# A mixture-of-experts stage on one core: gate and up products in 32-token groups on four column strips, and activations transposed on VectorE

## The reference

```
gate = jnp.minimum(xb @ w_gate[e] + b_gate[e], SWIGLU_LIMIT)
up = jnp.clip(xb @ w_up[e] + b_up[e], -SWIGLU_LIMIT, SWIGLU_LIMIT)
act = (up + 1.0) * gate * jax.nn.sigmoid(SWIGLU_ALPHA * gate)
return act @ w_down[e] + b_down[e]
```

## Time and profile before

| | |
|---|---|
| runs | 2298.77 us median of 3 (2298.28 to 2299.28) |
| span of the profiled execution | 2300.9 us |
| PE busy | 2168.5 us (94%) |
| DVE busy | 1023.7 us (44%) |
| ACT busy | 478.9 us (21%) |
| POOL busy | 452.8 us (20%) |
| HBM read, written | 482.08 MB, 32.51 MB |

### The profile page before, as it was taken

The page is one execution under the profiler, slowest core; times in us unless marked ns, Lnnn a source line. Parts: engine busy times, 40 slices in busy tenths (PEclk is TensorE's granted clock), DMA queues, the critical chain, the costliest instruction groups (busy, mean ns, idle before and its releaser), DMA issues.

```text
span 2300.9 us, 35458 instructions
## 1 busy us (share of the span) xinstructions
PE 2168.5 (94%) x9927; PEld 1011.6 (44%) x9928; DVE 1023.7 (44%) x1591; ACT 478.9 (21%) x647; POOL 452.8 (20%) x422
## 2 busy tenths in 40 slices
PE   6999999789959999999999899999999999999995
PEld 3544444564534444443443344444444444444442
DVE  2765656657772432534335243433254333222346
ACT  2343347422210111111011111111111111111134
POOL 0011100002321222323122232212213212212212
PEclk9999999889969999999999999999999999999998
DMA  9222320022245776789479999747899647897673
GB/s 352 80 63 76 101 73 19 3 107 87 82 193 186 263 271 221 268 305 393 146 281 399 351 353 402 268 162 252 300 373 345 235 160 261 292 320 247 206 280 130
DMA packets 169785, 512.34 MB, mean 223 GB/s; under 512 B 16815, under 2 KB 51383, under 8 KB 168586
## 3 DMA queue, kind: packets, MB, share of 16 engines
q1 hardware_dynamic: 152290, 468.96, 54.7%
q0 software_dynamic: 15840, 37.45, 7.3%
q10 hardware_dynamic: 1608, 5.29, 0.6%
HBM read 482.08 MB, written 32.51 MB: 224 GB/s over the span
## 4 chain that ended last, share of the span: by engine, by line
PE 87%; DVE 5%; DMA 3%; SPq 2%; issue 2%; ACT 1%; POOLq 0%; POOL 0%; DVEq 0%; ACTq 0%
PE psall L587 27%; PE psall L615 14%; PE psall L591 10%; PE psall L772 9%; PE psall L596 5%; PE psall L619 5%; PE psall L760 3%; PE psall L879 2%; PE psall L873 2%; PE psall L624 2%; DMA arena<-in_w_down_dram 2%; PE psall L656 1%; PE psall L739 1%; SPq L437 1%; DVE arena L1498 1%
## 5 line engine op out<-in xcount | busy, mean ns | idle before, releaser
L587 PE MATMUL psall<-arena 128*128 128x512 f32 x1472 | 645.5, 597 | 23.9 <-issue 18.7
L587 PEld LDWEIGHTS psall<-arena 128*128 128x128 f32 x1472 | 278.6, 191 | 369.2 <-issue 362.5
L615 PE MATMUL psall<-arena 128*128 128x512 f32 x736 | 322.6, 596 | 4.8 <-issue 2.7
L591 PE MATMUL psall<-arena 128*64 128x512 f32 x1152 | 256.1, 595 | 6.2 <-issue 2.5
L1670 DVE STREAM_TRANSPOSE arena<-arena 128x1024 f32<-128x1024 f32 x49 | 61.0, 1246 | 447.4 <-PE psall L587 276.5
L772 PE MATMUL psall<-arena 128*128 128x512 f32 (+1 forms) x560 | 227.1, 562 | 0.0
L615 PEld LDWEIGHTS psall<-arena 128*128 128x128 f32 x736 | 139.2, 191 | 182.6 <-issue 180.8
L1256 ACT COPY arena<-psall 128x512 f32<-128x512 f32 x49 | 28.7, 586 | 729.1 <-PE psall L656 729.1
L1869 DVE COPY arena<-psall 128x512 f32<-128x512 f32 x48 | 33.2, 692 | 310.7 <-PE psall L656 303.0
L1268 ACT ACTIVATE arena<-arena 128x1024 f32<-128x1024 f32 x49 | 51.8, 1057 | 569.3 <-DVE arena L1697 556.0
L1652 DVE TENSOR_TENSOR arena<-psall,arena 32x256 f32<-32x256 f32 (+2 forms) x122 | 78.6, 644 | 195.5 <-PE psall L615 137.5
(11 more groups left out here) (332 smaller groups left out, 2130.4 us busy)
## 6 DMA issues: line engine op xcount, KB each, us to landing
arena<-in_w_gate_dram SPq DMA_DIRECT2D x128, 1024.0 KB
arena<-in_w_up_dram SPq DMA_DIRECT2D x128, 1024.0 KB
arena<-in_w_down_dram SPq DMA_DIRECT2D x128, 1024.0 KB
arena<-in_w_ada_dram SPq DMA_DIRECT2D x16, 1024.0 KB, 5.2
arena<-in_w_ada_dram SPq DMA_DIRECT2D x4, 2048.0 KB, 14.7
arena<-in_x_dram SPq DMA_DIRECT2D x16, 512.0 KB, 6.8
arena<-in_w_in_dram SPq DMA_DIRECT2D x16, 512.0 KB, 4.0
arena<-in_w_out_dram SPq DMA_DIRECT2D x1, 4096.0 KB, 13.8
```

The lines of the kernel that those rows point to most:

```text
L587: mm = pe.matmul(ps[2 * g + s], xT[:, k, :], w[:, s * BANK:(s + 1) * BANK], start=(k == 0), stop=(k == KD - 1))
L591: mm = pe.matmul(ps[2 * g][HT * j:HT * j + HT, :], xT[:, k, 0:HT], w[:, j * BANK:(j + 1) * BANK], start=(k == 0), stop=(k == KD - 1), skip ...
L615: mm = pe.matmul(ps[6 + s], aT[:, k, :], w[:, s * BANK:(s + 1) * BANK], start=(k == 0), stop=(k == KD - 1))
```

## The change

PE computes gate and up for every kind in the same way. The tokens are taken in groups of 32. For a group t, the four quarters of the hidden columns go to the four column strips, and the moving operand of one product is 256 gate columns and 256 up columns together, 512 in all, read as two pieces (`wpair`, which is the ring seen as four pairs of a gate and an up piece). The result of a group fills one PSUM bank, gate in the first half and up in the second (`psGU`, four banks). Kind 4 has 128 such products where it had 32, kind 3 has 96, kind 2 has 64 and kind 1 has 32.

DVE then adds the biases with one instruction each over 256 columns a group, on all 128 partitions, for every kind. The activations stay in strips: partition 32j+s, column 256t+n holds token 32t+s and hidden column 256j+n. `turn_activations` transposes them in 32x32 blocks with a read step of eight columns, so that partition p of `aT` holds hidden columns 8p to 8p+7. The down weights are loaded to match: eight consecutive rows of `w_down` on each partition, two of them a piece, in runs of 8 KB. PE's transposes, their PSUM banks and the copies of ACT and DVE are gone.

The order within a turn is new. PE: gate and up of job u in one block, then down of job u-1. The block begins when both sums of job u-1 have been read from PSUM (`gu_free`), where before the gate part waited for `g_biased` alone and the up part for `gu_free`. DVE: rows of the next job, `swiglu` of u, `weigh` of u-1, and then the turn of the activations of u, since `aT` is in use until the down product of u-1 ends. PE gives a gate and an up piece free together. SP issues the gate and up pieces of the next expert first, then waits for `gu_free` and loads its two bias rows straight to 128 partitions (`ebq`: quarter j of the row to partitions 32j to 32j+31, 1 KB each), then the down pieces. POOL broadcasts the down bias row alone.

```diff
+        ebq = reg(o, 2, QW); o += 512
+        ebd = reg(o, D); o += 1024
...
+        wpair = [reg(4096 * m, 2, 2, D) for m in range(NPAIR)]
+        brow = adarow[0:1, 2, :]
...
-        psG, psU = psall[:, 0:2 * BANK], psall[:, 2 * BANK:4 * BANK]
-        psT, psY = psall[:, 4 * BANK:6 * BANK], psall[:, 6 * BANK:8 * BANK]
+        psGU = psall[:, 0:4 * BANK].rearrange("p (t g n) -> p t g n", t=4, g=2)
+        psY = psall[:, 6 * BANK:8 * BANK]
...
-                    if u is not None:
-                        sp.wait_ge(gu_used, GUP * u + (q + 1))
+                    if u is not None and q % 2 == 0:
+                        sp.wait_ge(gu_used, NPAIR * u + (q // 2 + 1))
...
-                    w_v = w_down[0].rearrange("e (q c p) n -> e q p c n", c=2, p=P)[:, q]
+                    w_v = w_down[0].rearrange("e (p q c) n -> e q p c n", q=DNP, c=2)[:, q]
...
-                    sp.dma_start(brow[:, g * D:(g + 1) * D], b_v[0][ds(e, 1)]).then_inc(d_bias, 16)
+                    rows = b_v[0][ds(e, 1)].rearrange("a (j n) -> (a j) n", j=4)
+                    sp.dma_start(ebq[:, g], rows.unsqueeze(1).to_broadcast([4, QR, QW])).then_inc(d_bias[g], 16)
...
-                            spread = sp.value_load(tab[0:1, ds(u * NC + (NC + J_ORD), 1)], min_val=16, max_val=16 * NE)
-                            sp.wait_ge(bias_spread, spread)
-                            settle(sp)
+                            gu_pieces(e, u)
+                            sp.wait_ge(gu_free, u + 2)
                             bias_rows(e)
-                            gu_pieces(e, u)
...
-        def gate_up(pe, kind, u, order_, k0, k1, first=False):
-            if k0 == 0:
+        def gate_up(pe, groups, u, order_, m0, m1):
+            if m0 == 0:
                 pe.wait_ge(xT_ready, u + 1)
-            sweeps = {4: ("full",), 3: ("half", "quarter"), 2: ("half",), 1: ("quarter",)}[kind]
-            for sweep in sweeps:
-                for q in range(k0, k1):
-                    g = q % 2
-                    if q < 2 and sweep == sweeps[0]:
-                        if g == 0 and not first:
-                            pe.wait_ge(g_biased, u)
-                        if g == 1:
-                            pe.wait_ge(gu_free, u + 1)
-                    if sweep == sweeps[0]:
-                        pe.wait_ge(d_gu[q], order_)
-                        if kind < 4:
-                            settle(pe)
-                    for k in (2 * (q // 2), 2 * (q // 2) + 1):
-                        w = ring[q][:, k % 2]
-                        if sweep == "full":
-                            for s in range(2):
-                                mm = pe.matmul(ps[2 * g + s], xT[:, k, :], w[:, s * BANK:(s + 1) * BANK],
-                                               start=(k == 0), stop=(k == KD - 1))
-                        if sweep == "half":
-                            for j in range(2):
-                                mm = pe.matmul(ps[2 * g][HT * j:HT * j + HT, :], xT[:, k, 0:HT], w[:, j * BANK:(j + 1) * BANK],
-                                               start=(k == 0), stop=(k == KD - 1), skip_group_check=True)
-                        if sweep == "quarter":
-                            r = slice(QUARTER_AT[kind], QUARTER_AT[kind] + QR)
-                            for j in range(4):
-                                mm = pe.matmul(ps[2 * g + 1][QR * j:QR * j + QR, 0:QW], xT[:, k, r], w[:, j * QW:(j + 1) * QW],
-                                               start=(k == 0), stop=(k == KD - 1), skip_group_check=True)
-                    if sweep == sweeps[-1]:
-                        mm.then_inc(gu_used, 1)
+                pe.wait_ge(gu_free, u + 1)
+            for m in range(m0, m1):
+                for q in (2 * m, 2 * m + 1):
+                    pe.wait_ge(d_gu[q], order_)
+                    settle(pe)
+                for k in (2 * m, 2 * m + 1):
+                    for t in range(groups):
+                        for j in range(4):
+                            mm = pe.matmul(psGU[QR * j:QR * j + QR, t], xT[:, k, QR * t:QR * t + QR],
+                                           wpair[m][:, :, k % 2, QW * j:QW * j + QW],
+                                           start=(k == 0), stop=(k == KD - 1), skip_group_check=True)
+                mm.then_inc(gu_used, 1)
 
         def down(pe, kind, u, order_):
-            pe.wait_ge(aT_act, u + 1)
-            pe.wait_ge(aT_dve, u + 1)
+            pe.wait_ge(aT_ready, u + 1)
...
                             t, on_ = typ_of(pe, typ_c), ord_of(pe, ord_c, wait_c)
-                            by_kind(pe, t, lambda kind: gate_up(pe, kind, u, on_, 0, GUP // 2))
+                            by_kind(pe, t, lambda kind: gate_up(pe, kind, u, on_, 0, NPAIR))
                             tp, op_ = typ_of(pe, typ_p), ord_of(pe, ord_p, wait_p)
-                            with pe.If(tp > 0):
-                                pe.wait_ge(act_ready, u + 1)
-                                by_kind(pe, tp, lambda kind: turn(pe, ub, JOB_KINDS[kind][2] // P, JOB_KINDS[kind][1] // P).then_inc(act_turned, 1))
-                                pe.nop()
-                            by_kind(pe, t, lambda kind: gate_up(pe, kind, u, on_, GUP // 2, GUP))
                             job_row(pe, [typ_n, ord_n], u + 2)
                             by_kind(pe, tp, lambda kind: down(pe, kind, u, op_))
...
-            def swiglu(u, kind):
-                parts, lo, hi = JOB_KINDS[kind]
+            def swiglu(u, groups):
                 s7 = 1.0 / (1.0 + math.exp(-SWIGLU * LIMIT))
-                dve.wait_ge(gu_used, u * GUP + GUP)
-                dve.wait_ge(bias_spread, order_)
-                for p0, p1, c, b, n in parts:
-                    mm = dve.tensor_tensor(gb[p0:p1, c:c + n], psG[p0:p1, c:c + n], ebias[p0:p1, 0, b:b + n], ALU.add)
-                mm.then_inc(g_biased, 1)
-                for p0, p1, c, b, n in parts:
-                    mm = dve.scalar_tensor_tensor(out=ub[p0:p1, c:c + n], in0=psU[p0:p1, c:c + n], scalar=1.0,
-                                                  in1=ebias[p0:p1, 1, b:b + n], op0=ALU.add, op1=ALU.add)
-                mm.then_inc(gu_free, 1)
-                w = slice(lo, hi)
+                w = slice(0, QW * groups)
+                gv, uv = (v[:, w].rearrange("p (t n) -> p t n", t=groups) for v in (gb, ub))
+                bias = [ebq[:, g].unsqueeze(1).to_broadcast([P, groups, QW]) for g in range(2)]
+                dve.wait_ge(gu_used, u * NPAIR + NPAIR)
+                dve.wait_ge(d_bias[0], order_)
+                dve.tensor_tensor(gv, psGU[:, 0:groups, 0], bias[0], ALU.add).then_inc(g_biased, 1)
+                dve.wait_ge(d_bias[1], order_)
+                dve.wait_ge(aT_ready, u + 1)
+                dve.scalar_tensor_tensor(out=uv, in0=psGU[:, 0:groups, 1], scalar=1.0, in1=bias[1],
+                                         op0=ALU.add, op1=ALU.add).then_inc(gu_free, 1)
                 dve.wait_ge(gu_free, u + 2)
...
+            def turn_activations(u, groups):
+                dve.wait_ge(act_ready, u + 2)
+                dve.wait_ge(dn_used, u * DNP + DNP)
+                dve.transpose(aT[:, :, 0:QR * groups].rearrange("p b (t s) -> p t b s", s=QR),
+                              ub[:, 0:QW * groups].rearrange("p (t i b) -> p t b i", i=QR, b=KD)).then_inc(aT_ready, 1)
...
                                     by_kind(dve, tp, lambda kind: weigh(u, kind, orderp))
+                                    by_kind(dve, typ_of(dve, typ_c), lambda groups: turn_activations(u, groups))
```

65 lines of the change are left out of this document (21 added, 44 removed).

## The result

| | us, median (range) | runs |
|---|---|---|
| before | 2298.65 (2298.28 to 2299.28) | 4 |
| after | 2773.0 (2761.53 to 2792.16) | 4 |
| ratio | 1.2067, 95% interval 1.2028 to 1.2106 | |

The account below looks back on a forecast made before the run. PE's own work bounds most of the expert stage, the weights' arrival some 200 us. -7-37-6+2+2+3+8+4 = -31 off the 2298.77 us median gave 2268 us, own range 2254 to 2280, overall 2250 to 2318.

Parts of the forecast that it names:

- the loop, once fetched, stays with the engine: PE's job loop: no instruction packets after 780 us in the profile before, so no refetching; 0 us in the sum.
- Rival A: PE's grown loop is refetched every pass: +32 (2300 us) with one packet, +130 (near 2398) with several; chance 0.10 each.
- The price of a fetch: Instruction packet of 16 KB for PE: put at 2 us, an estimate between 0.7 us and three times it.
- The bias rows: Gate and up bias to 128 partitions, 0.7 us an expert by DMA; +4 with the later request of the first down piece.
- my terms ahead of it: Products -7, PE transposes -37, issue gaps -6, DVE's turn +2, start +2, waits for weights +8.
- The 8 for weights: Full DMA stretches, where PE's savings only make it wait for weights: +8 us given back.
- The rate of four strips: PE's gate and up products, 512 columns on four strips: 108 ns an instruction, 112 as upper bound; products -7 us.
- rival B: PE's strips slow each other at 512 columns, 112 ns an instruction: 2307 us, slower; chance 0.07.
- The issue gaps: PE's waits for branches and table loads ahead of blocks: -6 of 18 us, between 0 and -12.
- The end: Last down block, now behind weigh of the job before and the turn (1.25 us) on DVE: +3 us.
- Rival C: Saturated weight stretches widen, by pairwise ring release or bias packets on few engines: another 12 to 20, 2283 us; chance 0.14.
- The 144 groups of 32: Token groups from 288 transposes at two per 32 tokens, used to get 8, 10 and 8 jobs of kinds 3, 2, 1.

Follow-up runs that it names:

- after_3as4: The changed kernel with kind 3 running kind 4's gate and up products in the loop, its own code removed; 2352.17 us, ratio 1.0222.
- after_cut: The changed kernel without one never-executed piece of code ahead of the loop, which then starts 69 instructions earlier; 2701.96 us, ratio 1.172.
- before_pad24: The kernel before with 24 never-executed products (96 instructions) added in the job loop; 2972.99 us, ratio 1.2933.
- before_pad88: The kernel before with 88 never-executed products (352 instructions) added in the job loop; 3047.58 us, ratio 1.3257.
- one_code: The changed kernel with one code for all kinds' gate and up products, groups 1 to 3 behind tests of the kind; 2330.71 us, ratio 1.0121.
- bias_wide: one_code with the bias rows brought in by eight requests of 32 partitions in place of two of 128; 2302.26 us, ratio 1.0.
- bias_late: one_code with the bias rows and the wait for gu_free moved behind the down pieces on SP's queue; 2316.84 us, ratio 1.0062.
- bias_none: one_code without the gate and up bias rows of all experts but the first, and without waits for them; 2271.06 us, ratio 0.9861.

## Why the prediction was wrong

**The step that failed** is that the loop, once fetched, stays with the engine. Rival A named the mechanism and the point from which it decides, and the packets of 256 in the loop (5.9 to 7.1) were worked out, but it got a chance of 0.20 in all, on the ground that nothing shows where the store ends. The rule cited there from the Trainium skill ("Runtime: NRT & Kernel Launch", "Instruction fetch mechanics") gives a store of 2048 instructions in blocks of 256; by that the loop and one block ahead are 9 blocks where 8 fit. The runs bear it out to the block: loops of 7 blocks stay (before, after_3as4), loops of 8 don't (after, after_cut, before_pad24), and before_pad24 and before_pad88 fetch, in the mean of all passes, their blocks and nearly one more. In the prediction's own terms, the sum had 0 for instruction fetches, and they cost 442 us. Rival A ought to have been the forecast.

**The size of rival A** was off in one factor. The price of a fetch was put at 2 us and measures 1.5 to 1.8. The count was put at one or two a pass, "at each jump"; it is 4.9 in the mean, and 8.9 in before_pad24, where nearly every block is entered in every pass: a loop that is one block too long loses more than the block that doesn't fit. 248 x 1.78 = 442 us, not 130.

**The bias rows** are the term of the sum that was mis-sized: +4, measured 61 in one_code. I priced their packets by their share of 16 engines, 0.7 us an expert. Not in that price: the few packets under way at a time (30 us, bias_wide), and SP's wait for VectorE and its two requests (7.7 us for the pair at 1060 us), both in front of the down pieces (16 together, bias_late). The remaining part of the 61 is not divided. The rule of the Trainium skill ("DMA: Bandwidth & Descriptors", section on why a DMA increments its semaphore by 16) by which 4 source rows go to 4 engines, which I had set at 12 to 15 us and left out of the sum, agrees with the mean width of the bursts, 3.3 packets in the median, and with bias_wide, whose gain is twice that price. It is not proven by them: at the peak of a burst up to 8 packets are under way at once in one_code and 20 in bias_wide, so the packets under way are not a count of engines.

**The other terms held.** Without instruction fetches and bias transfers the kernel takes 2271.06 us, 31.7 less than its before; the forecast was 31 less with 4 for the bias, so 35 less without. The last but one down block starts 34.7 us earlier in bias_none than in before; my terms ahead of it (-7 - 37 - 6 + 2 + 2 + 8) make -38. The 8 for weights is 8.7 (waits of 19.8 us against 11.1). The rate of four strips was right: 256 instructions take 27.6 us in one_code, as many as in the earlier trace rows for twice 32 full ones, so rival B falls. The issue gaps are 7 to 8 us in place of 18, where I took 6 off. The end costs 4.8 us more than before (from the 48th down block to the last instruction 48.4 against 43.6), and I had 3: the turn is 2.05 us where the same operation on rows takes 1.25. The turn reads columns with a step of 8; that this is the reason was not tried apart. The last down block in one_code, behind VectorE's turn, beside the earlier trace rows:

```profile
2295.97 15.71 PE L608 MATMUL psall<-arena 128*128 128x512 f32 x32 [10.05 <-DVE arena L1696]
```

```profile
2290.08 1.72 DVE L1631 TENSOR_TENSOR arena<-psall,arena 32x256 f32<-32x256 f32 x4
2291.92 1.95 DVE L1636 SCALAR_TENSOR_TENSOR arena<-arena,lruw,adarow 32x256 f32<-32x256 f32 x4
2293.90 2.01 DVE L1696 STREAM_TRANSPOSE arena<-arena 128x1024 f32<-128x1024 f32 x1
```

Rival C (2283, the weights) came true in kind, at 61 us where it had 12 to 20 beyond the forecast. Of its two causes it was the bias packets, and not the release in pairs. In after itself none of it shows beside the fetches: waits for weights are 38.6 us there.

One step of the working proves nothing, though its result was right. The 144 groups of 32 follow from the 23, 18 and 16 whatever the number of kind-3 jobs, so they can't give it; the 49 jobs do: 23 + 18 + 16 - 49 = 8. The turns by width above (22, 8 and 10 from 760 us on, and 8 of kind 1) agree with 8, 10 and 8.

## What to carry to other kernels

Count the instructions of the longest loop of the busiest engine in blocks of 256 at their place in the program, all branches included, before any change that makes them more. Here 7 blocks stayed and 8 did not; one block too many made nearly all of them be fetched again in every pass of before_pad24, and code that never runs counted in full. The profile has an early sign, the instruction queue's packets against the stretch in which they fall. A small transfer is priced not by its bytes alone but by how many of its packets are under way at a time, the wait ahead of it on its queue, and the time its request holds that queue, which differed more than tenfold here.

## What was not expected of the hardware

- A hundred instructions more in a loop (1518 to 1618), 96 of them never executed, took a kernel from 2298.31 to 2972.99 us. It has 435 instruction packets of 16 KB more, and all its 465 are 1.2% of the DMA engines' time.
- The same 275 packets cost 71 us less (2773.0 to 2701.96) when the loop was moved by 69 instructions.
- One request for 128 packets of 1 KB held SP for 0.63 us at 857 us and for 8.12 us at 1388 us (one_code), with the DMA full at both.
- DVE's STREAM_TRANSPOSE of 1024 columns took 2.05 us where its columns are read with a step of 8, and 1.25 for the rows of tokens; 0.65 for 256 columns.
